# Prompt attention: the float32 probabilities move from SBUF into the scores' PSUM bank

## The reference, cut to what matters

```python
logits = einsum('bqhd,bkhd->bhqk', q, k) * scale + cq - ck      # scale = 64 ** -0.5
logits = where(key <= query, logits, -inf)
probs  = softmax(logits)
out    = einsum('bhqk,bkhd->bqhd', probs, v)
```

## Time and profile before

| what | value |
|---|---|
| three runs, median (lowest to highest) | 1980.89 us (1978.67 to 1981.26) |
| the profiled execution, own time | 1982.06 us |
| its span, first to last instruction | 1980.2 us |
| prompt attention, first to last instruction | about 1100 to 1547 us |
| busy share of the span: PE, DVE, ACT, POOL | 96%, 66%, 43%, 12% |

### The profile page before, as it was taken

The page is one execution under the profiler, slowest core; times in us unless marked ns, Lnnn a source line. Parts: engine busy times, 40 slices in busy tenths (PEclk is TensorE's granted clock), DMA queues, the critical chain, the costliest instruction groups (busy, mean ns, idle before and its releaser), DMA issues. The chain is left out here.

```text
span 1980.2 us, 28779 instructions
## 1 busy us (share of the span) xinstructions
PE 1894.0 (96%) x10726; PEld 1732.3 (87%) x10726; DVE 1310.9 (66%) x2127; ACT 846.6 (43%) x1529; POOL 230.0 (12%) x165
## 2 busy tenths in 40 slices
PE   4999999999999999999999999999999899999998
PEld 3899999999999999999999777777777699998886
DVE  7788888955455465444655688889987544455654
ACT  4454555534343442433323576666678710111100
POOL 4000000000000000000000202333323520000111
PEclk9999999999999999999999899999999999999999
DMA  5599898969888886879897715566554598665441
GB/s 182 199 305 321 286 309 306 299 233 303 290 290 296 288 299 193 300 238 312 264 295 249 159 42 105 120 129 126 121 102 137 168 340 277 212 209 153 138 142 68
DMA packets 272750, 435.99 MB, mean 220 GB/s; under 512 B 63236, under 2 KB 139156, under 8 KB 268476
## 3 DMA queue, kind: packets, MB, share of 16 engines
q1 hardware_dynamic: 272612, 434.16, 70.0%
HBM read 285.18 MB, written 148.78 MB: 219 GB/s over the span
## 5 line engine op out<-in xcount | busy, mean ns | idle before, releaser
L751 ACT ACTIVATE fr_wq<-fr_raw 128x512 fp32r<-128x512 f32 x288 | 178.0, 625 | 200.8 <-PE fr_d L617 137.0
L1665 DVE TENSOR_TENSOR at_p_lo<-at_p,at_p_hi 128x512 fp32r<-128x512 f32 (+1 forms) x320 | 228.0, 721 | 42.3 <-ACT at_p_hi L1635 41.7
L1634 ACT ACTIVATE at_p<-at_s 128x512 f32<-128x512 f32 (+1 forms) x320 | 170.6, 533 | 116.1 <-PE at_s L1558 68.1
L615 PE MATMUL fr_b<-fr_xh,fr_wq 128*128 128x348 f32 x576 | 189.0, 328 | 14.0 <-DVE fr_u L1120 10.5
L1009 DVE TENSOR_TENSOR fr_wq<-fr_raw,fr_wq 128x512 fp32r<-128x512 f32 x288 | 192.8, 684 | 8.7 <-ACT fr_wq L751 5.0
L615 PE MATMUL fr_c<-fr_xh,fr_wq 128*128 128x348 f32 x576 | 187.0, 325 | 4.4 <-DVE fr_wq L1009 2.5
L615 PE MATMUL fr_a<-fr_xh,fr_wq 128*128 128x348 f32 x576 | 187.9, 326 | 2.4 <-DVE fr_wq L1009 1.8
L616 PE MATMUL fr_a<-fr_xl,fr_wq 128*128 128x348 f32 x576 | 187.2, 325 | 0.0
L617 PE MATMUL fr_a<-fr_xh,fr_wq 128*128 128x348 f32 x576 | 186.6, 324 | 0.0
L617 PE MATMUL fr_b<-fr_xh,fr_wq 128*128 128x348 f32 x576 | 186.3, 323 | 0.0
L616 PE MATMUL fr_b<-fr_xl,fr_wq 128*128 128x348 f32 x576 | 186.3, 323 | 0.0
(11 more groups left out here) (314 smaller groups left out, 4578.5 us busy)
## 6 DMA issues: line engine op xcount, KB each, us to landing
fr_wq<-w_mixed SPq DMA_DIRECT2D x192, 512.0 KB, 5.6
fr_raw<-w_tiles SPq DMA_DIRECT2D x96, 512.0 KB, 5.5
w_mixed<-fr_wq SPq DMA_DIRECT2D x96, 512.0 KB, 4.6
mg_gates<-merge_gates SPq DMA_DIRECT2D x40, 416.0 KB, 4.6
fr_raw<-w_tiles SPq DMA_DIRECT2D x48, 256.0 KB, 5.5
merge_gates<-fr_res SPq DMA_DIRECT2D x32, 348.0 KB, 6.7
mixed<-mg_mixed SPq DMA_DIRECT2D x40, 208.0 KB, 3.8
ln_h<-h_rows SPq DMA_DIRECT2D x16, 512.0 KB, 3.3
```

The costliest lines, as they stand in the source:

```text
L615: pe.matmul(to, wh[:, idx, k, :], xh[:, idx, k, :], start=first, stop=False, skip_group_check=skip)
L751: act.activation(wh[:, idx], operand(i, idx), ACT.Copy).then_inc(w_hi[idx], 1)
L1634: act.activation(p[:, r, cols], s_bank[r][:, cols], ACT.Exp, scale=SCALE)
L1665: dve.tensor_tensor(p_lo[:, r, cols], p[:, r, cols], p_hi[:, r, cols].bitcast(F32), ALU.subtract)\
```

## The change

ACT computes the rounded exponential first, into `p_hi` as before. Then it computes the float32 one and writes it over the scores, into the bank that it reads. DVE's subtraction reads the bank and `p_hi`. The buffer `p` (8 KB per partition) is gone and nothing takes its place.

The bank is now in use until DVE has read it, so PE's wait before it writes new scores into a bank is on `lo_done` (DVE's count) instead of `p_done` (ACT's). The initial credit of four moves with it from one semaphore to the other, and the sample's first user of these banks waits for `lo_done` too.

```diff
-        p = sb("p", [P, RING, QW], 28672)
...
-        st_.all_p, st_.all_pv, st_.all_read = (p_done, NS * H + RING), (pv_done, NS * H + RING), (o_read, NQ * H + 2)
+        st_.all_p, st_.all_pv, st_.all_read = (lo_done, NS * H + RING), (pv_done, NS * H + RING), (o_read, NQ * H + 2)
...
             def scores(h, b, st):
-                pe.wait_ge(p_done, NS * h + st + 1)
+                pe.wait_ge(lo_done, NS * h + st + 1)
...
             def values(h, b, st):
-                pe.wait_ge(lo_done, NS * h + st + 1)
+                pe.wait_ge(lo_done, NS * h + st + 1 + RING)
...
-            act.sem_inc(p_done, RING)
+            act.sem_inc(lo_done, RING)
...
             def probs(h, st):
-                act.activation(p[:, r, cols], s_bank[r][:, cols], ACT.Exp, scale=SCALE)
-                act.activation(p_hi[:, r, cols], s_bank[r][:, cols], ACT.Exp, scale=SCALE).then_inc(p_done, 1)
+                act.activation(p_hi[:, r, cols], s_bank[r][:, cols], ACT.Exp, scale=SCALE)
+                act.activation(s_bank[r][:, cols], s_bank[r][:, cols], ACT.Exp, scale=SCALE).then_inc(p_done, 1)
...
             def low(h, st):
-                dve.wait_ge(p_done, NS * h + st + 1 + RING)
-                dve.tensor_tensor(p_lo[:, r, cols], p[:, r, cols], p_hi[:, r, cols].bitcast(F32), ALU.subtract)\
+                dve.wait_ge(p_done, NS * h + st + 1)
+                dve.tensor_tensor(p_lo[:, r, cols], s_bank[r][:, cols], p_hi[:, r, cols].bitcast(F32), ALU.subtract)\
                    .then_inc(lo_done, 1)
```

## The result

The changed kernel takes **1956.67 us** (median of 4 runs, 1954.03 to 1960.04) against 1980.89 (4 runs, 1978.67 to 1981.26): a ratio of 0.9886, 95% interval 0.9872 to 0.9899, that is 20 to 25 us less. The profiled execution took 1960.04 us with a span of 1958.2, which is 22.0 less than the old span of 1980.2.

The account below looks back on a forecast made before the run. In the attention, PE and DVE were both taken as nearly full, with DVE's low parts waiting beside POOL and delaying PE. Gains of 20.4 and 3.2 us, 23.6 together, off 1980.89 gave 1957.3 us, range 1952 to 1965.

Parts of the forecast that it names:

- DVE's operand: Attention's low part, 512 columns: reading one PSUM operand, 0.69 us long beside POOL instead of 1.50.
- The stretch of the sample's attention: Old trace's low parts with a PSUM and an SBUF operand: 0.69 us while POOL subtracts for 11.43 us.
- The rule of the Trainium skill: DVE access overhead 60 ns on SBUF, 125 on PSUM: 65 ns more per low part, 2.6 us per head.
- Heads 1 to 6 at head 0's pace: 34 steps in each of heads 1 to 6 fall to head 0's 44.91 us: 23.2 us gained.
- What stays: Negated maximum (line 1681) still waits for POOL in heads 1 to 6: 2.8 us kept, ends 0 and 5.5.
- Head 7: Eight steps beside POOL go from 12.51 us to 1.16 each, PE becoming the limit: 3.2 us gained.
- ACT, PE's wait, DMA: Swapped exponentials, in-place PSUM write, PE's wait for the low part, and DMA loads: each taken as 0.
- The sum: Whole kernel: 20.4 us from heads 1 to 6 plus 3.2 from head 7, 23.6 us gained.
- rival 3: Low parts beside POOL: the contention stays, through `p_hi` or the output; total 1981 us, chance 0.04.
- Rival 1: Heads 1 to 6: PE meets another limit, only part gained; half gives 1969 us, chance 0.10.
- Rival 2: Second exponential, all 320 steps: in-place write pays columns twice, 14.4 us per head; about 1988 us, chance 0.04.
- Rival 4: DVE's low parts: PSUM costs 65 ns more each, 11 us over seven heads; 1968 us, chance 0.03.

Follow-up runs that it names:

- experiment 1: Kernel before, with POOL's twelve attention instructions per head in heads 1 to 7 replaced by clears that read nothing: 1954.1 us.
- experiment 3: Changed kernel, with the row maximum in a PSUM bank, from where the negated maximum reads it: 1951.64 us, ratio 0.9860.
- experiment 2: Changed kernel, with both operands of DVE's low part in SBUF (`p_hi` read twice, low parts become zero): 1975.51 us.
- experiment 4: Kernel before, with only the two exponentials swapped, both still written to SBUF: 1981.23 us.
- experiment 5: Changed kernel, with a third ACT instruction per step, an SBUF copy of up to 384 columns into an unread buffer: 1988.74 us.
- experiment 6: Changed kernel, with one more DVE instruction per step ahead of the low part, a maximum over 8 bank columns: 1964.74 us.

## Why the prediction was right, and where it was not

**DVE's operand: right.** 0.69 us was taken for a low part beside POOL, 0.682 measured; 24 to 25 us of low parts a head were expected, and the windows of `at_p_lo` alone, heads 2 and 7 of the changed kernel, have 23.9 and 24.4 (PE, PEld, DVE; as the earlier trace rows):

```profile
1211.05:1264.87 53.82, 14.61 (x41) 7.64 (x40) 23.91 (x41) 1.00 0.57 119
...
1480.06:1522.10 42.04, 15.01 (x42) 7.82 (x41) 24.39 (x40) 1.00 0.52 155
```

The stretch of the sample's attention was a short sample, but of the right form. The rule of the Trainium skill (Perfetto Trace Analysis, Optimizing Scalar/DVE Operations) was rightly not taken into the sum: experiments 1 and 3 run the same head at 44.93 and 44.95 us, with `p` in SBUF and in PSUM.

**Heads 1 to 6 at head 0's pace: right**, in every step but one (step 31). 23.2 us were to be had, 17.8 came, and the rest is that one step.

**What stays: mis-sized.** Half of the wait at line 1681, 2.8 us, was taken as kept. All of it was: 274.87 − 6 × 44.92 = 5.4, the term's own upper end (5.5). The argument was that POOL gets quicker and DVE comes earlier, so that they might miss each other. POOL did get quicker elsewhere and DVE did come earlier, but DVE met the same instruction of POOL, the eleventh of its twelve, in each of heads 1 to 6 and in both kernels, for 1.07 us in place of 0.94 in head 2. That instruction had no wait to lose: it took 1.29 us before too, and the 1.62 are another's. Its place does not hang on POOL's pace either. The subtraction just ahead of it waits for ACT's high part (idle 2.25 us in POOL's timeline above, 1.15 before), which ACT writes between its steps. So it moves with the steps, as DVE's maxima do, and a half between two ends was no reading of that order.

**Head 7: slightly under.** The eight steps went from 12.51 to 9.22 (9.3 expected), but the 34 steps gained 3.7 and not 3.2: other steps beside POOL had lost time too, and the prediction counted only one stretch. PE is the limit there now, as the prediction had it (windows of the changed kernel, head 7; columns as in the earlier trace rows):

```profile
1480.06:1521.77 41.71, 41.71 (x215) 34.43 (x214) 26.60 (x45) 37.06 (x82) 15.23 (x12) 1.00 0.52 156
```

**ACT, PE's wait, DMA: right, all at nothing.** The in-place bank took 591 ns by the nearer row and not the farther end; experiments 2 and 4 put ACT's whole side at 0.8 us or less over heads 1 to 6. No new wait stands in the chain.

**The sum** was 23.6; the change's own is 21.5, and the profiled pair shows 22.0 only because the stretches outside the change gave 3.9 and took 3.4. The first goes with the clock as its rows show; of the second the rows show a part (0.92 against 0.89), and the rest of its cause is open. That the median of the runs (1956.67) lies within a microsecond of the forecast (1957.3) is thus partly luck; the two mis-sized terms (2.6 too much, 0.5 too little) are smaller than the interval of the result.

**The rivals.** The contention left the low part (rival 3 falls by the earlier trace rows beside its row of after, and by experiment 2). Rival 1's named cause, the full wait at line 1681, did come true, but it costs 5.4 of the 23.2 us there, not half. Rival 2's price is of the right size: 1988 − 1957, some 31 us, were worked out, 24 stand in the stretches of experiment 5 (the 1988.74 of its run has the clock in it), and head 7, where 14.4 us more of ACT were to make it over 6 us longer than before, became 44.42 − 38.80 = 5.6 longer. Rival 4's was too high: it let 60% of an added DVE time show in seven heads, where experiment 6 has 23 to 30%.

## What to carry to other kernels

When the same instruction has two lengths in one trace, line the long ones up with what the other engines do at that moment, and look in the old trace for a stretch without it: head 0 gave the gain of six other heads to 0.03 us a step. If the partner is POOL reading SBUF, try an operand in PSUM for the DVE instruction, and do so for the small instructions too, where they stand ahead of PE's turn. A wait that the change doesn't touch is to be kept whole in the sum, unless the order of events shows why it should go.

## What the runs showed of the hardware

- A DVE instruction of 16 columns, one SBUF operand and an SBUF result, waits for POOL up to 1.07 us where it takes 0.17 alone; reading PSUM it takes 0.17 beside POOL too. The prediction had read this wait in the old trace, but it called only the case with two SBUF operands the contested one. The Trainium skill (SBUF — State Buffer, Who interferes with whom) has both: operations with two SBUF inputs contend with GpSimd's reads, and `tensor_scalar` may enter a mode that uses the shared ports. Experiments 1 to 3 agree, with the lengths given there; whether line 1680 was in such a mode no run shows. By the same section operations with two SBUF inputs don't contend with a GpSimd instruction that only writes; the 683 ns beside POOL's clears in experiment 1 agree with that as well.
- It goes both ways: POOL's products of line 1729 fell to 1.29 us in the mean (1.54 before, 1.62 for the one in the earlier trace rows), although nothing of POOL was edited.
- ACT reading and writing the same PSUM bank in place costs nothing measurable: 591 ns for 512 columns, against 594 with the result in SBUF.
- The stretch of about half the clock at the start of the attention ends at different times in executions of nearly the same work, though PE is fully busy (0.54 against 1.00 in the same seven microseconds, above; over steps 0 to 5 of head 0 it is 0.52 in the kernel before and 0.81 in experiment 4). That is worth 4 us of the total, a fifth of this change's gain. What sets its end is open: it was late in the traces of the kernel before and of experiment 5, and in none of the other eight, edits of either kernel.
